# Token-major x of a Mamba-2 layer: transposes on TensorE replaced by 32x32 block transposes on VectorE and a round trip through DRAM

## What is computed

```python
zxbcdt = h @ w_in                                  # z, (x, B, C), dt
xbc = silu(causal_dwconv(xbc, conv_w, conv_b))     # depthwise over time, 4 taps
xs = xbc[..., :D_INNER]                            # 4 groups of 8 heads of 64 channels
xdt = xs * dt                                      # chunks of 128 tokens
y_diag = einsum("bcgls,bcgrls,bcsgrp->bclgrp", cb, decay, xdt)
states = einsum("bclgn,bcgrl,bclgrp->bcgrpn", bc, decay_to_end, xdt)
y = y_diag + y_off + d_skip * xs                   # then gate by silu(z), group norm, w_out
```

## Time and profile before

| | us |
|---|---|
| median of 3 runs | 1108.34 (1108.01 to 1108.51) |
| the profiled execution | 1108.48 |
| its span in the profile | 1106.7 |
| PE busy | 1094.0 |
| POOL busy | 590.2 |
| DVE busy | 575.0 |
| ACT busy | 466.2 |

### The profile page before, as it was taken

One profiled execution on the slowest core, in us unless ns is written; L12 is line 12 of the kernel. 1 busy time (PEld: TensorE's weight loads), 2 busy tenths in 40 slices (PEclk: granted clock), 3 DMA queues, 4 the chain that ended last, 5 costly groups with the idle time before them and its releaser, 6 DMA issues.

```text
span 1106.7 us, 15323 instructions
## 1 busy us (share of the span) xinstructions
PE 1094.0 (99%) x5156; PEld 897.5 (81%) x5156; DVE 575.0 (52%) x644; ACT 466.2 (42%) x801; POOL 590.2 (53%) x447
## 2 busy tenths in 40 slices
PE   8999999999999999999999999999999999999997
PEld 6788888888888788788787878888888888888886
DVE  6755421455432384666777856665664224554123
ACT  7433222233333338458595785343332222333332
POOL 3766544454456635437364375656665444444653
PEclk9999999999999999999999999999999999999999
DMA  7222232322223325333324333222222222233232
GB/s 267 95 95 97 93 98 98 104 98 95 95 95 95 95 77 148 130 109 124 124 97 143 113 116 106 96 95 95 95 95 95 95 95 95 96 97 104 91 106 76
DMA packets 39941, 117.05 MB, mean 106 GB/s; under 512 B 4064, under 2 KB 11872, under 8 KB 39904
## 3 DMA queue, kind: packets, MB, share of 16 engines
q1 hardware_dynamic: 39472, 115.70, 31.4%
q10 hardware_dynamic: 432, 0.86, 0.2%
HBM read 114.32 MB, written 2.23 MB: 105 GB/s over the span
## 4 chain that ended last, share of the span: by engine, by line
PE 96%; DVE 1%; ACT 1%; issue 0%; DMA 0%; POOL 0%; DVEq 0%; ACTq 0%
PE bank L814 30%; PE bank L815 30%; PE bank L816 30%; PE bank L998 1%; PE bank L1007 1%; PE bank L1015 1%; PE bank L957 1%; PE bank L857 1%; DVE x_lo L1108 0%; DMA x_token<-x_tok 0%; ACT x_hi L482 0%; PE bank L975 0%; ACT residual L488 0%; PE bank L835 0%; DVE residual L1155 0%
## 5 line engine op out<-in xcount | busy, mean ns | idle before, releaser
L694 POOL TENSOR_TENSOR w_lo<-w_raw,w_hi 128x512 fp32r<-128x512 f32 x372 | 499.4, 1348 | 469.7 <-ACT w_hi L435 469.4
L435 ACT ACTIVATE w_hi<-w_raw 128x512 fp32r<-128x512 f32 x372 | 230.6, 626 | 404.0 <-PE bank L816 400.0
L814 PE MATMUL bank<-x_hi,w_hi 128*128 128x512 f32 x848 | 335.5, 396 | 2.7 <-DVE x_lo L1108 1.7
L816 PE MATMUL bank<-x_hi,w_lo 128*128 128x512 f32 x848 | 330.2, 389 | 0.0
L815 PE MATMUL bank<-x_lo,w_hi 128*128 128x512 f32 x848 | 330.1, 389 | 0.0
L814 PE MATMUL bank<-act_hi,w_hi 128*128 128x512 f32 (+1 forms) x656 | 254.2, 387 | 0.0
L816 PE MATMUL bank<-act_hi,w_lo 128*128 128x512 f32 (+1 forms) x656 | 251.9, 384 | 0.0
L815 PE MATMUL bank<-act_lo,w_hi 128*128 128x512 f32 (+1 forms) x656 | 251.8, 384 | 0.0
L814 PEld LDWEIGHTS bank<-x_hi,w_hi 128*128 128x128 f32 x848 | 159.2, 188 | 40.3 <-issue 6.1
L815 PEld LDWEIGHTS bank<-x_lo,w_hi 128*128 128x128 f32 x848 | 159.3, 188 | 34.1 <-issue 2.2
L816 PEld LDWEIGHTS bank<-x_hi,w_lo 128*128 128x128 f32 x848 | 159.2, 188 | 33.5
(11 more groups left out here) (153 smaller groups left out, 682.7 us busy)
## 6 DMA issues: line engine op xcount, KB each, us to landing
w_raw<-weights SPq DMA_DIRECT2D x186, 512.0 KB, 3.3
m<-acs_scratch SPq DMA_DIRECT2D x16, 512.0 KB, 4.2
decay_in<-eacs_scratch SPq DMA_DIRECT2D x24, 128.0 KB, 3.7
x_token<-x_tok SPq DMA_DIRECT2D x4, 512.0 KB, 6.9
residual<-xt SPq DMA_DIRECT2D x8, 256.0 KB, 9.9
out_first<-scaled_residual SPq DMA_DIRECT2D x4, 256.0 KB, 2.4
out_second<-output_rows SPq DMA_DIRECT2D x4, 256.0 KB, 2.7
pooling_matrices<-pooling ACTq DMA_DIRECT2D x1, 576.0 KB, 5.0
```

The lines of the kernel that those rows point to most:

```text
L435: act.activation(whi[:, c % 2, part], raw[:, c % 2, part], ACT.Copy).then_inc(hi_ready, 1)
L694: pool.tensor_tensor(wlo[:, c % 2, part], raw[:, c % 2, part], whi_f[:, c % 2, part], ALU.subtract).then_inc(lo_ready, 1)
L814: pe.matmul(out, wh, xh, start=start, stop=False)
L816: return pe.matmul(out, wl, xh, start=False, stop=stop)
```

## The change

x's token-major form is made in another way. DVE transposes the 32x32 blocks of each x tile into `yx` (which skip * x fills later), SP writes them with four DMAs of 32 partitions into a DRAM scratch, in rows of 512 bytes, waits until they have landed, and reads them back with one DMA so that tokens lie on the partitions. DVE then multiplies by dt in two instructions per chunk that also put the channels in order. ACT's skip moves from slot 0 to slot 3, behind the fourth x_dt. POOL's `decayed(g, 1)` moves behind the first half of a split. PE's waits for PSUM banks move with the transposes. The diff, with the declarations of semaphores and scratch left out:

```diff
...
+        def x_blocks(g):
+            return yx[:, GT * g:GT * g + GT, :].rearrange("p i t -> p (i t)").rearrange("p (n f) -> p n f", f=GT * Q)
...
+            def write_blocks(g):
+                sp.wait_ge(xt_blocks, g + 1)
+                blocks = x_blocks(g)
+                for a in range(P // Q):
+                    sp.dma_start(x_dram[g, :, :, a, :].rearrange("n q f -> q n f"),
+                                 blocks[Q * a:Q * a + Q, :, :]).then_inc(xt_written, 16)
+            def read_tokens(g):
+                sp.wait_ge(xt_written, 16 * (P // Q) * (g + 1))
+                sp.dma_start(yx[:, GT * g:GT * g + GT, :],
+                             x_dram[g].rearrange("(c b) q a f -> (b q) c (a f)", c=CHUNKS)
+                             ).then_inc(xt_landed, 16)
...
                 for t in range(slots(g)):
+                    if t == 0:
+                        write_blocks(g)
                     load_ahead(slot_of(g, t))
+                    if t == 0:
+                        read_tokens(g)
                     c = chunk_after.get(t)
...
-                act.wait_ge(x_act, g + 1)
+                act.wait_ge(xdt_ready, 4 * g + 4)
                 for i in range(GT):
...
                         first_tap(CONVS * (g + 1) + t - GT)
-                    if t == 0:
+                    if t == 3:
                         skip(g)
...
                         decayed(g, 0)
+                    split_half(U_SSM + u + 2, 0)
+                    if t == 2:
                         decayed(g, 1)
-                    split_half(U_SSM + u + 2, 0)
                     if t == T_STAT - 1 and g:
...
-            def token_x(g, c):
-                for i in range(GT):
-                    last = pe.transpose(XT_BANK[c][:, P * i:P * i + P], xact[:, i, P * c:P * c + P], ident)
-                last.then_inc(x_mm, 1)
...
                 if g:
-                    pe.wait_ge(xdt_ready, 4 * g)
+                    pe.wait_ge(bt_ready, g)
                 for c in range(CHUNKS):
...
                 last.then_inc(cb_mm, 1)
-                pe.wait_ge(x_act, g + 1)
-                if g == 0:
+            def c_chunk(g, c):
+                return cf[:, g % 2, P * c:P * c + P]
+            def chunk(g, c):
+                pe.wait_ge(m_ready, 4 * g + c + 1)
+                pe.wait_ge(xdt_ready, 4 * g + c + 1)
+                if g == 0 and c == 0:
                     pe.wait_ge(acsf_ready, 1)
                 else:
-                    pe.wait_ge(y_add, 4 * g)
-                    pe.wait_ge(y_dec, 3 * g)
-                    pe.wait_ge(state_ready, 3 * g)
-                for c in range(CHUNKS - 1):
-                    token_x(g, c)
-            def c_chunk(g, c):
-                return cf[:, g % 2, P * c:P * c + P]
-            def chunk(g, c):
-                pe.wait_ge(m_ready, 4 * g + c + 1)
-                pe.wait_ge(xdt_ready, 4 * g + c + 1)
-                if c:
                     pe.wait_ge(y_add, 4 * g + c)
...
                     pe.wait_ge(state_ready, 3 * g + c)
-                    if c > 1:
+                    if g or c > 1:
                         pe.wait_ge(y_dec, 3 * g + c - 1)
...
                     pe.wait_ge(bt_ready, g + 1)
-                    if c == 0:
-                        pe.wait_ge(xdt_ready, 4 * g + 3)
+                    if g and c == 0:
+                        pe.wait_ge(state_ready, 3 * g)
                     pe.matmul(b_st[:, :], bt[:, c, :], dec[:, c % 2, :], start=True, stop=True).then_inc(st_ready, 1)
...
                         token_major(g)
-                    if t == T_LATE_TOKEN:
-                        pe.wait_ge(bt_ready, g + 1)
-                        token_x(g, CHUNKS - 1)
                     if t == T_STAT and g:
...
+            def transpose_blocks(g):
+                dve.wait_ge(x_act, g + 1)
+                blocks = x_blocks(g)
+                for i in range(GT):
+                    last = dve.transpose(blocks[:, :, Q * i:Q * i + Q],
+                                         xact[:, i, :].rearrange("p (n j) -> p n j", j=Q))
+                last.then_inc(xt_blocks, 1)
...
-                dve.wait_ge(x_mm, 4 * g + c + 1)
-                dve.tensor_tensor(by_head(xdt[:, c, :]), by_head(XT_BANK[c][:, :]),
-                                  of_group(dt_t[:, :, :].rearrange("p c h -> p (c h)"), c, g, HD), ALU.mult
-                                  ).then_inc(xdt_ready, 1)
+                dve.wait_ge(xt_landed, 16 * (g + 1))
+                if g and c == 0:
+                    dve.wait_ge(yd_ready, 4 * g)
+                    dve.wait_ge(dec_ready, 3 * g)
+                out = xdt[:, c, :].rearrange("p (i h a j) -> p h i a j", h=2, a=2, j=Q)
+                landed = yx[:, GT * g + c, :].rearrange("p (h a i j) -> p h i a j", h=2, a=2, j=Q)
+                dt = dt_t[:, c, HPG * g:HPG * g + HPG].rearrange("p (i h) -> p h i", h=2)
+                for half in range(2):
+                    last = dve.tensor_tensor(out[:, half], landed[:, half],
+                                             dt[:, half].unsqueeze(2).unsqueeze(3).to_broadcast([P, GT, 2, Q]),
+                                             ALU.mult)
+                last.then_inc(xdt_ready, 1)
...
                         after_chunk(g - 1, CHUNKS - 1)
+                    if t == 1:
+                        transpose_blocks(g)
                     if t == 1 and g:
...
                         masked_cb(g)
-                        token_x(g, 0)
-                        token_x(g, 1)
-                        token_x(g, 2)
-                    if t == 3:
-                        token_x(g, 3)
                     if t == T_STAT + 1 and g:
...
                     if t == 2:
+                        token_x(g, 0)
+                        token_x(g, 1)
                         decay_times_cb(g, 0)
+                        token_x(g, 2)
+                        token_x(g, 3)
                     if t == T_NORM and g:
...
```

More of the change, by code:

```diff
@@ L56 @@
 TIMES_CB_IN = {4: 1, 6: 2, 8: 3}
-T_TOKEN, T_LATE_TOKEN = 1, 2
+T_TOKEN = 1
+Q = 32
 T_STAT, T_NORM = 4, 7
@@ L182, in build @@
         acs_dram = nc.dram_tensor("acs_scratch", [GROUPS, CHUNKS, HPG, P], F32).ap()
+        x_dram = nc.dram_tensor("x_scratch", [GROUPS, CHUNKS * (P // Q), Q, P // Q, GT * Q], F32).ap()
         eacs_dram = nc.dram_tensor("eacs_scratch", [GROUPS, CHUNKS, HPG, P], F32).ap()
@@ L188, in build @@
         b_misc, b_yd, b_yo, b_st, b_stat = bank[3], bank[4], bank[5], bank[6], bank[7]
-        XT_BANK = (b_yd, b_yo, b_st, b_misc)
         x_landed = [sem(f"x_landed{m}") for m in range(KD)]
@@ L248, in build @@
         cb_mm = sem("cb_product")
-        x_mm = sem("x_transposed")
+        xt_blocks = sem("x_blocks_transposed")
+        xt_written = sem("x_blocks_written")
+        xt_landed = sem("x_token_major_landed")
         xdt_ready = sem("x_dt_ready")
@@ L977, in token_major @@
                 last.then_inc(cb_mm, 1)
-                pe.wait_ge(x_act, g + 1)
-                if g == 0:
-                    pe.wait_ge(acsf_ready, 1)
-                else:
-                    pe.wait_ge(y_add, 4 * g)
-                    pe.wait_ge(y_dec, 3 * g)
-                    pe.wait_ge(state_ready, 3 * g)
-                for c in range(CHUNKS - 1):
-                    token_x(g, c)
             def c_chunk(g, c):
@@ L994, in chunk @@
                 pe.wait_ge(xdt_ready, 4 * g + c + 1)
-                if c:
+                if g == 0 and c == 0:
+                    pe.wait_ge(acsf_ready, 1)
+                else:
                     pe.wait_ge(y_add, 4 * g + c)
```

## The result

The changed kernel takes 1141.6 us against 1108.07 us, a ratio of 1.0302 (95% interval 1.029 to 1.0313): 33.5 us slower, where 9.8 were forecast, and above the range. Its profiled execution has a span of 1140.5 us (before 1106.7), so 33.8 us are to be found. (One execution of the changed kernel read 1839.87 us and is left out as disturbed.)

The account below looks back on a forecast made before the run. TensorE's issuing of matmuls was taken to bound the kernel. Groups 0 to 3 gave +4.8, 0, +2.5 and +2.5, the saved 6.3 included: 1108.48 + 9.8 = 1118.3 us, range 1105 to 1134.

Parts of the forecast that it names:

- The blocks: DVE's four transposes of x, 0.6 us each, done at 428.7, 496.6, 567.4 and 635.7 us in groups 0 to 3.
- The writes: Four DMAs of 512-byte rows to DRAM, 1 MB a group: 6.6 us (4.4 to 8.4), SP's issuing 3.6 of it.
- Group 0's stall: TensorE's stall before chunk 0 of group 0, 6.4 us, with the writes queued behind decay_in and other DMA traffic.
- By bytes: Rival: the DRAM trip costs by bytes, T = 12.2, about 0 us change, 1108.5 us; chance 0.14.
- hidden: Rival: the whole DRAM trip is hidden before chunk 0, four groups at -1.6 us, 1102.2 us; chance 0.10.
- Read: The 1 MB DMA back from DRAM in 2 KB packets: 4.8 us (4.4 to 6.5, if it shares the queue).
- DVE behind it: After the read lands: four x_dt instructions, then m, with two semaphore hops, 3.2 us (2.7 to 4.2).
- Clock: TensorE's clock may fall after a stall: 0 to 2 us a stall, taken as 0, in the upper end.
- T: Time from transposed blocks to m for chunk 0: 6.6 + 4.8 + 3.2 = 14.6 us (12.2 to 19.1).
- my first rival: Trip costs by rows in a shared queue, DVE held up beside POOL: T = 19.1, 1137 to 1140 us; chance 0.16.
- the saved 6.3 us: TensorE's transposes of x removed, 1.6 us a group in four groups: the whole gain there can be.
- my third rival: The whole DRAM trip is hidden, when T falls to 10.5 us: 1108.5 - 6.3 = 1102.2 us; chance 0.10.

Follow-up runs that it names:

- the dummy matmuls: Changed kernel plus 25, 22, 36 and 36 extra matmuls on TensorE ahead of chunk 0 of groups 0 to 3; 1136.58 us, ratio 1.0268.
- that kernel: Changed kernel with m of chunk 0 ahead of x_dt, and no slot 4 weight tile before the read nor DMA behind it until landed; 1128.67 us.
- the last version: Against the kernel before: TensorE still transposes chunk 0's x, only chunks 1 to 3 go through DRAM; 1105.52 us, ratio 0.9977.
- the kernel with the clear road: Changed kernel, no slot 4 weight tile issued ahead of the x read nor anything behind it until it has landed; 1129.21 us, ratio 1.0189.
- the kernel with long rows: Changed kernel with one write of 8 KB rows instead of four of 512-byte rows, and four short-row reads instead of one; 1136.11 us, ratio 1.0247.

## Why the prediction was wrong

**Right.** The bound, the place and the kind: line 1012 waiting for DVE's m, four times, and nothing else of size. The blocks: with the time gained and lost in earlier groups taken off (a group's stall and slow stretch less 1.6: 6.9, then 13.6, then 23.8 us), they are ready at 496.5, 567.5 and 635.9, forecast 496.6, 567.4 and 635.7; transposes 0.62 us apart, forecast 0.6. The writes: 6.4 us, forecast 6.6, though in other parts (SP 3.1, not 3.6). Group 0's stall, 6.35 against 6.4, was luck: there the writes were 3 us quicker through the queue than I had them, and read and DVE ate that. "By bytes" and "hidden" are out, by row cost: the writes move at 204 GB/s with the engines 0.89 busy, where the Trainium skill (DMA: Bandwidth & Descriptors, Anatomy of one DMA and Specifications) has a fit with 436 GB/s, taken on DMAs that GpSimd issues, and line rate from 512 bytes on. For these writes, issued by SP, the trace does not agree.

**Wrong, in three terms.**
- *Read*, 4.8 us forecast, 7.5 to 8.2 measured in groups 1 to 3 (6.4 in group 0). The step that failed: "there is no other traffic beside this read but one weight load", and the share of the queue kept for the upper bound (6.5). That load stands ahead and still runs when the read is issued. Alone the read takes 5.3, with the load ahead 7.0, with what stands behind it as well 7.8. Excess 2.8 us a group in the mean.
- *DVE behind it*, 3.2 forecast (up to 4.2), 4.5 measured. I priced x_dt at the pace of an instruction that reads PSUM, 0.42 us for 256 columns; 2.28 us for four is 0.57 each, and m took 2.29, not 1.59. Both have their operands in SBUF: the first three x_dt, begun while POOL waited, took 0.42 us each, the fourth and m ran beside POOL. And I took the order x_dt, x_dt, m as given instead of asking whether m could go first; moved alone it is worth 14 us. Excess 1.3 us.
- *Clock*, 0 to 2 us a stall, taken as 0. Rows 11 had shown the grant falling under 2 us after the last matmul; here it fell 4.0 to 4.5 us into the idle time, and a stall of 5.7 to 9.2 us cost 2.1 to 2.7 us more. About 10 us, of which the dummy matmuls show only 5 to be recoverable.

Read and DVE make T 3.9 to 4.7 us longer in groups 1 to 3, and the stalls come to 30.3 us against 16.2, 14 us more; with the clock's 10 that is the 24 us between +9.8 and +33.8. T = 19.1, the value of my first rival (0.16), was near the measured 18.5 to 19.3, and with "a fallen clock some 4 more" it missed only by the clock. Of its three reasons two held, the shared queue and DVE beside POOL; 54 ns a packet did not, it was about 36.

**What the saved 6.3 us are worth.** In this kernel they are in the time in full, as the account above shows. Where no stall sets the end they are not to be had: taken alone they are worth 4.4, and 0.6 (within the noise) once DVE does the transposes and skip has moved. So even with the trip hidden my third rival's 1102.2 would not have come. "DVE bounds nothing, so I count them only where they stand in the new path" missed that transposes and moved skip delay the gate, and ACT's exponentials and m with it. "Nothing" for POOL's and ACT's new waits held as long as the stall covered them; with m ahead of x_dt a first bit came out, 0.8 us for w_lo in two waits. (The 2.69 us above come from the late weight tile of that kernel.)

## What to carry to other kernels

Price a DMA that other work waits for from the moment when the transfers *issued before it* have landed, and look at what the wait for it leaves to do on the critical engine: work that does not need the transfer goes ahead of it in that engine's program. A producer moved from a saturated engine to an idle one pays with a deadline, so move only the part whose deadline is far, as the last version does. A stall as long as these (5 to 9 us) is priced with the slow matmuls behind it, and mending one wait is checked against what it had been covering.

## What the runs showed of the hardware

- DVE's multiplication of two SBUF operands goes with what POOL does. Both rows are of the changed kernel (duration in ns, shortest, median, longest):

```profile
L1329 DVE TENSOR_TENSOR x_dt<-y_accumulated,dt_token x32: 418/1262/1504, 443.5 to 682.9; 128x256 f32<-128x256 f32 x32
...
L1315 DVE STREAM_TRANSPOSE y_accumulated<-x_conv x16: 668/671/711, 426.3 to 659.0; 128x512 f32<-128x512 f32 x16
```

  The same instruction takes 418 ns at the least and 1262 in the median, three times as much; in groups 0 and 1 the first three, begun while POOL waited for them, took 418 to 426 ns, and the next, beside POOL, 1265. The transposes, with one SBUF operand, stay between 668 and 711 ns, though POOL is busy throughout those of groups 2 and 3; multiplications from PSUM take 680 ns for twice the columns. The Trainium skill (SBUF — State Buffer, Who interferes with whom) has such a rule: a DVE instruction with two SBUF inputs contends with a GpSimd instruction that reads SBUF; one with at most one, outside the 2-port modes, does not. The trace agrees. That POOL is the cause is read off the stretches in which it waits; no run stopped it for that purpose.
- 2048 packets of 512 bytes cost about 36 ns each: in the kernel with the clear road the DMA share between 500 and 506 us adds up to 4.6 us of 16 engines. One write of 1 MB in 8 KB rows moved at 350 GB/s together with the start of a weight tile (the kernel with long rows, 507 to 510 us), where these moved at 204.
- A read of 1 MB in 2 KB rows lands in 5.3 us alone, 7.0 with one 512 KB tile ahead of it, 7.8 with traffic behind it as well (medians of four).
